# Paired projections of a gated delta-rule layer as 2x2 block products with seven multiplications instead of eight

## The reference

```
p   = h @ w_in                                   # 1024 -> 6208, all tokens
qkv = silu(centred_dwconv(p[..., :4096], conv_w)) # depthwise, 4 taps
z   = p[..., 4096:6144]                          # gate path, used as silu(z)
q   = l2norm(q) * 128 ** -0.5 ; k = l2norm(k)    # 8 heads of 128
v   -> 16 heads of 128                           # two v heads share a q/k head
o   = gated_delta_chunked(...)                   # forward and backward in time
y   = (rmsnorm(o) * silu(z)) @ w_out
```

## Time and profile before

| | |
|---|---|
| median of 3 runs | 3240.86 us (3240.34 to 3242.18) |
| profiled execution, first to last instruction | 3251.1 us |
| PE, DVE, ACT, POOL busy | 95%, 53%, 47%, 27% of the span |
| layer 0, slots -1 to 14 | 205.4 to 1133.8 us of the span |
| layer 3, slots -1 to 14 | 2235.0 to 3071.2 us |

### The profile page before, as it was taken

One profiled execution on the slowest core, in us unless ns is written; L12 is line 12 of the kernel. 1 busy time (PEld: TensorE's weight loads), 2 busy tenths in 40 slices (PEclk: granted clock), 3 DMA queues, 4 the chain that ended last, 5 costly groups with the idle time before them and its releaser, 6 DMA issues. The chain is left out here.

```text
span 3251.1 us, 55663 instructions
## 1 busy us (share of the span) xinstructions
PE 3092.5 (95%) x21673; PEld 2016.4 (62%) x21673; DVE 1731.2 (53%) x3543; ACT 1539.1 (47%) x3296; POOL 873.2 (27%) x652
## 2 busy tenths in 40 slices
PE   5889999999999999999999999897999999999998
PEld 3357777777777764455445555444777777777753
DVE  1156666666666652244443334346676767776632
ACT  3155555555555531256432444335655565555521
POOL 0044434533533410011001101003544435343400
PEclk9699999999999999999999999898999999999999
DMA  9921111211211126022311111102212222121135
GB/s 375 330 68 54 56 56 55 67 56 45 72 56 51 45 89 235 1 68 64 128 33 31 29 46 52 72 4 80 66 53 69 59 60 63 57 68 53 43 120 192
DMA packets 224097, 261.93 MB, mean 81 GB/s; under 512 B 19418, under 2 KB 158948, under 8 KB 223716
## 3 DMA queue, kind: packets, MB, share of 16 engines
q1 hardware_dynamic: 223844, 258.46, 24.7%
HBM read 239.15 MB, written 19.27 MB: 79 GB/s over the span
## 5 line engine op out<-in xcount | busy, mean ns | idle before, releaser
L898 PE MATMUL ps<-hT,W 128*128 128x512 f32 (+1 forms) x2656 | 1001.2, 506 | 3.0 <-DVEq L192 2.0
L898 PEld LDWEIGHTS ps<-hT,W 128*128 128x128 f32 x2656 | 470.5, 193 | 195.1 <-issue 165.6
L1331 DVE CAST_PREDICATED arena<-mask,ps 128x384 bf16<-128x384 uint32 x448 | 253.2, 565 | 223.2 <-PE ps L967 174.3
L1148 ACT CAST arena<-ps 128x384 bf16<-128x384 f32 x384 | 166.9, 482 | 347.7 <-PE ps L954 346.7
L2372 PE MATMUL ps<-arena 128*128 128x512 f32 x712 | 311.2, 595 | 2.3 <-SPq L192 2.0
L1333 DVE CAST_PREDICATED arena<-mask,ps 128x384 bf16<-128x384 uint32 x448 | 250.9, 560 | 0.0
L2372 PEld LDWEIGHTS ps<-arena 128*128 128x128 f32 x712 | 134.5, 191 | 167.1 <-issue 162.8
L2007 PE MATMUL ps<-hT,W 128*128 128x512 f32 (+1 forms) x608 | 218.2, 493 | 0.6 <-DMA W<-in_att_w_in 0.4
L1455 POOL TENSOR_TENSOR arena<-arena 128x768 f32<-128x768 f32 (+1 forms) x32 | 44.4, 1389 | 636.0 <-ACT arena L1192 636.0
L1268 DVE SCALAR_TENSOR_TENSOR arena<-arena,vec 128x770 f32<-128x770 f32 (+1 forms) x192 | 205.4, 1070 | 6.8
L967 PEld LDWEIGHTS ps<-arena 128*128 128x128 bf16 x2304 | 144.7, 98 | 55.4 <-issue 51.0
(11 more groups left out here) (284 smaller groups left out, 6177.0 us busy)
## 6 DMA issues: line engine op xcount, KB each, us to landing
arena<-in_ada_w SPq DMA_DIRECT2D x24, 2048.0 KB, 19.5
W<-in_gdn_w_in SPq DMA_DIRECT2D x95, 512.0 KB, 4.0
arena<-decay_sums SPq DMA_DIRECT2D x64, 384.0 KB, 4.1
W<-decay_rows SPq DMA_DIRECT2D x64, 384.0 KB, 5.0
arena<-in_gdn_w_out SPq DMA_DIRECT2D x32, 512.0 KB, 10.5
W<-in_gdn_w_out SPq DMA_DIRECT2D x30, 512.0 KB, 3.4
arena<-gated SPq DMA_DIRECT2D x32, 384.0 KB, 7.7
gated<-arena SPq DMA_DIRECT2D x24, 384.0 KB, 2.3
```

The costliest lines, as they stand in the source:

```text
L898: mm = pe.matmul(ps[:, b, 0:t1 - t0], w[:, i, :], env.hT[:, i, t0:t1], start=(i == 0), stop=(i == KD - 1))
L1148: act.copy(half_cols(Xb[d], s, d), ps[:, 2 * d, 0:384].rearrange("p (c b s) -> p c b s", c=NT, s=s)).then_inc(*inxe.up(m, lv, d))
L1331: dve.copy_predicated(half_cols(Mb[d], s, d), wide(env.m4[:, d, lv]), src_m).then_inc(*inm.up(m, lv, d, "m"))
```

## The change

Two projections of 128 output channels each (k and q of one head, or v and z of one unit) over T tokens are one product of a 2x2 block matrix of weights (two tiles by two halves of the 1024 channels) with a 2x2 block matrix of hidden states (two halves of the channels by two halves of the tokens). It is formed with seven block products instead of eight (`strassen`). Pair A is the q tile h and k tile h, h = 1..7; pair B is v and z of unit m = 1..15; the first tiles stay as they were. In layer 0 a half of the tokens is 384, in layer 3 it is 256 of the latent ones; there the 256 context tokens of k and v stay ordinary fills (`c0`, `c1`). A block product is four matmuls (eight instructions) into one bank. Those of a chain (`CHAIN`: A1, A6; A5, A3; A7, A4; B1, B6, B5, B3; B7, B4) accumulate one upon the other in the same bank, and each intermediate sum is copied out by ACT before PE goes on in that bank.

- ACT copies every product out to SBUF, and DVE adds it afterwards to what it belongs to (`add`, one step after PE finished it, at the end of DVE's step). Silu of z becomes one instruction per slot on the sum (`gates`).
- POOL forms the sums of weights: `b_sums` (3 instructions of 128x512) and `b_last` (1) per unit, `a_sums` (3) and `a_last` (1) per pair A, and four sums of hidden states per layer. They lie in what was the space of `env.x`, which is reloaded by DMA before the output phase (from a copy in DRAM in layer 3).
- The convolution of k or q is done half in step 7, half in step 8; that of v half in step 13, half in step 14 behind the norm. `silu_v` moves to step 15, `gates` stands behind it. The table load back to exp/log stands directly behind `silu_x`.
- Some constants are loaded only for layer 2.

The core of the diff:

```diff
+CHAIN = {"A6": "A1", "A3": "A5", "A4": "A7", "B6": "B1", "B5": "B6", "B3": "B5", "B4": "B7"}
+ADDED = ("A2", "A5", "A3", "A7", "A4", "B2", "B7", "B4")
+KD2 = KD // 2
+def slot_order(n, last):
...
+    elif odd:
+        order = ["A7"] * heads + (["c1"] * fresh if last else o[:1]) + ["A4"] * heads + ["B1"] * fresh + (o if last else o[1:])
+        order += ["B6", "B2", "B5", ("B7", 0, 1), "B3"] * fresh
+    else:
+        if last:
+            order = ["c0", "A5", "A2", "A3"] * heads + o + ["B1", "c1", "B6", "B2", "B5", ("B7", 0, 1), "B3"] * fresh
+        else:
+            order = ["A5", "A2", "A3"] * heads + o[:1] + ["B1"] * fresh + o[1:] + ["B6", "B2", "B5", ("B7", 0, 1), "B3"] * fresh
+    small = (["x1"] if short else ["x0", "x1"]) * tile + ["G0", "G1"] * tile + ["k0", "k1"] * (tile and odd) + ["t0", "t1"] * unit
+    spare = [("B7", i, i + 1) for i in range(1, KD2)] * fresh + [("B4", i, i + 1) for i in range(KD2)] * fresh
+    if odd and n + 1 < 2 * GH - 2:
+        spare += [(use, i, i + 1) for use in ("A1", "A6") for i in range(KD2)]
...
+        def strassen(n, use, i, o):
...
+            elif i == 0 and which != 2:
+                form = {6: 2, 5: 1, 3: 4, 7: 3, 4: 3}[which]
+                sig, key = (aform, h) if kind == "A" else (bform, m)
+                pe.wait_ge(sig.sem, sig.at(key, form))
...
+            w, x = {1: (first[:, i], env.hT[:, i, H0]), 2: (first[:, KD2 + i], env.hT[:, KD2 + i, H0]),
+                    3: (first[:, KD2 + i], env.hT[:, KD2 + i, H1]), 4: (second[:, KD2 + i], h4[:, i]),
+                    5: (sum1[:, i], env.hT[:, i, H1]), 6: (sum2[:, i], h2[:, i]), 7: (second[:, i], h3[:, i])}[which]
+            return pe.matmul(o, w, x, start=(i == 0 and use not in CHAIN), stop=(i == KD2 - 1), skip_group_check=(use in CHAIN))
...
-            if n == -1 or last and n > -2:
+            if n > -2:
+                hold(env, act)
+                act.preload_act_table_set(LNEXP)
+
+        def gates(m):
+            act.wait_ge(dev.sem, dev.at(m - 1, "B4"))
+            sz = v.sz[:, m % 2, LO:T]
+            act.activation(sz, sz, ACT.Silu).then_inc(*zsd.up(m))
...
-                if p == 14 and m in U:
+                if p == (15 if n >= 0 else 14) and m in U:
                     silu_v(m)
+                if p == 15 and n in U and n:
+                    gates(n)
...
                 if p == 7 and n in TILES and n > -2:
-                    conv_x(n)
+                    conv_x(n, True, False)
+                if p == 8 and n in TILES and n > -2:
+                    conv_x(n, False)
...
+                if p == 14 and m in U and not (n >= 0 and step_at(n, "B3") == 13):
+                    conv(1, 16 + m, convv, m, 0, False)
+                for key in late[n, p]:
+                    add(*key)
...
+        def a_last(h):
+            kb = env.W[:, 0, KD2:]
+            pool.wait_ge(ad.sem, ad.at(2 * h - 2, "A2"))
+            pool.wait_ge(aform.sem, aform.at(h, 2))
+            pool.tensor_tensor(kb, kb, SUMS["A"][1], ALU.subtract).then_inc(*aform.up(h, 4))
```

355 lines of the change are left out of this document (265 added, 90 removed).

## The result

The changed kernel takes 3495.01 us (median of 4 runs, 3490.88 to 3505.17) against 3241.52 for the kernel before beside it: 1.078 times the time, 95% interval 1.0755 to 1.080. That is 254 us slower; I had forecast 89 us slower. The sign was right, the time lies outside the range, and the slowdown is nearly three times the forecast one. So the two profiles lie 242 us apart, 12 less than the medians.

What follows compares the result with a forecast made beforehand. The prediction took the kernel to be bound by what PE issues. Its terms, -95 + 49 + 26 + 68 + 18 + 11 + 36 - 24 = +89, gave a median of 3330 us, range for 8 in 10: 3235 to 3390.

Steps and rivals of the forecast that it cites:

- A: PE's fill matmuls: seven products instead of eight save 2.58 us per pair in layer 0, 1.72 in layer 3; -95 us.
- B: Chained products wait in their bank for ACT's copy without other fills as cover; +49 us (43 to 56).
- C: Step 9 of layer 3's odd slots: B3 waits for B5's copy behind ACT's Silu and table loads; +26 us.
- E: A2 to A3: PE waits for POOL's `a_last`, 1.3 us each, 14 times; +18 us.
- G: Step 11: half a convolution and adds on DVE make the merge and PE's next level late; +36 us (19 to 60).
- D: Steps 15 and 16: copies for G0, G1, A6 stand behind a table load and Silus on ACT; +68 us.
- F: A7 to A4 in layer 0's odd slots: A7's copy comes late behind L1143, 1.6 us 7 times; +11 us.
- Hidden: Work taken to cost nothing: POOL's sums of hidden states and weights, the reload of x, table loads unchanged in number.
- rival 1: POOL and DVE stop each other, also slowing C, F and G: +38 on the forecast, 3368 us; chance 0.19.
- rival 2: Backlogs are absorbed: C, D and G cost nothing, bare turns remain; -47, 3194 us; chance 0.21.
- H: Earlier waits that go, in layer 3's odd slots and layer 0's even ones; -24 us.
- rival 3: A wash: C, D and G at 47, sum 0, 3241 us; chance 0.06 together with the rest.

Runs made afterwards that it cites:

- e14: Changed kernel with silu_v and gates as copies of 16 elements on ACT from slot 4 on (output not the reference's): 3481.8 us, ratio 1.0736.
- e2: Changed kernel with silu_v and gates behind the copies of step 15 on ACT: 3504.4 us, ratio 1.0789.
- e4: Changed kernel with POOL's sums of weights cut from 512 to 64 elements per partition from unit 3 and pair 2 on: 3414.2 us, ratio 1.0506.
- e7: Kernel before, with PE waiting in step 9 of six odd slots of layer 3 for ACT's Silu behind two further table loads: 3274.3 us, ratio 1.0087.
- e8: Kernel before, with PE waiting in step 9 of layer 3's slots 1 to 12 for ACT's Silu, no further table loads: 3287.8 us, ratio 1.0135.
- e1: Changed kernel with silu_x and its table loads behind the copies of step 9 on ACT: 3479.7 us, ratio 1.0724.
- e5: Changed kernel with silu_x behind step 9's copies, A7's copy ahead of L1269, last adds behind matrix, and convolutions whole again: 3462.4 us, ratio 1.0675.
- e10: Changed kernel with POOL's sums and DVE's adds narrowed, silu_x behind step 9's copies, A7's copy earlier, last adds behind matrix: 3359.9 us, ratio 1.034.

## Why the prediction was wrong, point by point

- **A** was right: a 384-column instruction starts every 0.322 us.
- **B, C, E, G** were right in place and size (49, 27, 23, 39 us against 49, 26, 18, 36). In B there is some luck: a turn measured 0.73 and 0.63 us where I had 0.85 and 0.76, and the long ones from B4 to A1 were 1.63 and 1.19 where I had 1.26 and 0.95.
- **D** was right in size (52 of 68) and half wrong in cause. I put it down to ACT's Silus throughout; e14 shows that this holds for layer 3's odd slots alone, and that DVE's norm and subtraction end the others. Removing the Silus from ACT's order (e2) only moved the wait.
- **F** was priced at 1.6 us and is 4.05. The step that failed is "DVE now has adds of two halves near it, some 0.8 each": the add takes 1.82, beside POOL's square of the output, and the two instructions of `matrix` take 3.64 instead of 1.82, beside the sums of weights. e4, without most of the sums, has 2.22 us left here.
- **Hidden** is the step that failed most in work: "the weights' sums ... stand in POOL's free 70%". They do, but a DVE operation with two SBUF operands that meets one takes up to twice its time (`matrix` 1.82 us instead of 0.91). I had put this at nothing, and e4 prices the sums at 81 us. I had this as rival 1 and gave it 38, because I let it act on C, F and G alone and thought half a slot free on both engines would keep them apart. Of the waits that no term held, about 51 us, e4 removes the two largest of layer 3 (1.58 at a slot's start, 0.91 in step 9), some 15 us; the 0.73 and 0.77 of layer 0 stay as they were. Neither the sum nor rival 1 had the other part of this: the convolutions and adds, at their new places, meet work that POOL had before.
- **The clock** was in no term and in no rival, +50 us net. I priced each wait at its length. Waits between 1.6 and 4.4 us were followed, though not always, by 1.7 to 2.8 us lost at half clock, and e7 and e8 show that a wait alone brings this on. With it e1's gain is understood, and rival 2 could not have held either: it left waits of 1.6 us standing.
- **H** was about right; that the waits of the kernel before would vanish inside the new ones was true, but it hid that the odd slots of layer 3 had no slack left in DVE.

- **The median.** "It lies 10.2 us above the median of the runs, which carries over" did not hold: the profiled execution of the changed kernel lies 2 us below its median. That is 12 us of the miss.
- A slip in **rival 3**: with C, D and G at 47 the sum is +6, not 0, unless B is taken at its lower end, 43, where the forecast has 49. Nothing hangs on it.

By the table, then, of the 165 us missed about 50 are the clock, 17 term F, 51 waits without a term, 12 the first slots and 12 the median, against 16 us in which D was too dear; A, E and G add some 13, and 25 I can't assign. e4 says that the part of F above its forecast is mostly the sums', and about 15 of the 51. The effects overlap (e5, e10), so they can't be added as if each stood alone. That the table of causes is closed is not shown.

## What to carry to other kernels

Work saved on the engine that is the bound is worth its time only if the engine does not wait longer for what replaces it: count the handovers first, each at what the trace shows for a turn (0.73 us here, against 2.58 us saved per pair), and only then the columns. Look behind each wait of PE for a stretch at half clock, and add it where it is there. An engine with 70% of its time free is not free if its operations stop those of another: look at one row in which the two overlap and price the new work at that duration. The same holds for old work that is moved: ask which instruction of the other engine the same semaphore releases.

## What the runs showed of the hardware

- A wait of PE of 1.62 us, put into the kernel before with nothing else changed, was followed by 1.6 us lost at a granted clock of 0.5 in five slots of e8 and by nothing in a sixth; one of 2.92 us by 1.5 to 1.7 in four slots of e7 and by 2.3 and 3.1 in two; in the changed kernel a slot with one of 4.4 us and a later one of 3.1 lost 4.5.
- The same slots with the same waits lost 1 us in one profile and 3 in another (slots 1 to 3 of layer 0, changed kernel and e1).
- DVE beside POOL: `matrix`, 768 columns with two SBUF operands, 0.95 us alone and 1.8 to 2.0 in the overlap; an add of 128 columns 1.50 on average. With one operand in PSUM (L1492, L1483) 0.90 to 0.95 in either kernel.
- A turn of a bank between two products (PE to ACT to PE): 0.73 us for 384 columns, 0.63 for 256, about 0.43 for 16.
